# The second half of an output projection turned round: tokens on partitions, added and normalized piece by piece

## What is computed

```python
def rmsnorm(x, gain):
    y = x * lax.rsqrt(jnp.mean(x * x, axis=-1, keepdims=True) + RMS_EPS)
    return y * gain
...
mix = jnp.concatenate([y_rwkv, y_attn], axis=-1)   # 1024 x 2048
x = x + mix @ w_out[l]                             # w_out is 2048 x 2048
return rmsnorm(x, final_gain)
```

## Time and profile before

| | us |
|---|---|
| time, median of 3 runs | 1854.89 (1854.79 to 1863.19) |
| time of the profiled execution | 1853.96 |
| its span | 1852.0 |
| TensorE busy | 1821.9 (98%) |
| VectorE busy | 1242.8 (67%) |
| ScalarE busy | 815.3 (44%) |
| GpSimd busy | 476.8 (26%) |

### The profile page before, as it was taken

How to read it: one execution, slowest core, us unless ns; L and a number is a source line. 1 busy time by engine, 2 the same in 40 slices (tenths; PEclk the granted TensorE clock), 3 DMA queues, 4 the chain that set the end, 5 groups by cost and what they waited for, 6 DMA issues and landing times.

```text
span 1852.0 us, 37362 instructions
## 1 busy us (share of the span) xinstructions
PE 1821.9 (98%) x14560; PEld 1489.1 (80%) x14560; DVE 1242.8 (67%) x2239; ACT 815.3 (44%) x1690; POOL 476.8 (26%) x1096
## 2 busy tenths in 40 slices
PE   8999999999999999999999999999999999999996
PEld 5778888888888887888888888888888778888885
DVE  4676777777777678667777777787678753356433
ACT  6435444443535355444444535353544543242221
POOL 0005061423324150051423324050505060111110
PEclk9999999999999999999999999999999999999998
DMA  6533332333333335333433333333333543465433
GB/s 183 163 114 103 91 93 87 96 91 94 91 91 92 97 92 179 107 89 86 104 85 95 90 92 99 90 87 93 101 96 104 172 117 108 126 206 182 153 120 125
DMA packets 194960, 207.65 MB, mean 112 GB/s; under 512 B 98272, under 2 KB 101472, under 8 KB 194784
## 3 DMA queue, kind: packets, MB, share of 16 engines
q1 hardware_dynamic: 194784, 205.26, 38.9%
HBM read 183.18 MB, written 22.02 MB: 111 GB/s over the span
## 4 chain that ended last, share of the span: by engine, by line
PE 85%; POOL 4%; DVE 4%; DMA 3%; issue 2%; SPq 1%; ACT 1%; DVEq 0%; POOLq 0%; ACTq 0%
PE psum L1206 70%; PE psum L1191 3%; POOL sub_io L520 2%; POOL sub_t L518 2%; PE psum L1330 2%; PE psum L1270 1%; PE psum L1480 1%; PE psum L1298 1%; PE psum L1363 1%; PE psum L1444 1%; PE psum L1451 1%; DMA sub_l<-scratch_L 1%; PE psum L1215 1%; DMA w_raw<-in_w_in 1%; PE psum L1232 1%
## 5 line engine op out<-in xcount | busy, mean ns | idle before, releaser
L1206 PE MATMUL psum<-x_hi,w_hi 128*128 128x512 f32 x2144 | 870.7, 406 | 9.2 <-DVE x_lo L788 6.2
L1206 PE MATMUL psum<-x_hi,w_lo 128*128 128x512 f32 x2144 | 838.4, 391 | 0.0
L1206 PE MATMUL psum<-x_lo,w_hi 128*128 128x512 f32 x2144 | 838.0, 391 | 0.0
L779 DVE TENSOR_TENSOR w_lo<-w_raw,w_hi 128x512 fp32r<-128x512 f32 x536 | 372.5, 696 | 491.3 <-ACT w_hi L563 462.4
L563 ACT ACTIVATE w_hi<-w_raw 128x512 fp32r<-128x512 f32 x536 | 335.4, 629 | 740.2 <-PE psum L1206 631.8
L1206 PEld LDWEIGHTS psum<-x_hi,w_hi 128*128 128x128 f32 x2144 | 403.5, 188 | 108.5 <-issue 13.7
L1206 PEld LDWEIGHTS psum<-x_hi,w_lo 128*128 128x128 f32 x2144 | 403.0, 188 | 87.2
L1206 PEld LDWEIGHTS psum<-x_lo,w_hi 128*128 128x128 f32 x2144 | 404.0, 188 | 79.9 <-issue 4.4
L518 POOL TENSOR_TENSOR sub_t<-sub_l,sub_io 128x60 f32<-128x60 f32 (+24 forms) x496 | 192.8, 389 | 876.9 <-DMA sub_l<-scratch_L 839.3
L520 POOL TENSOR_TENSOR sub_io<-sub_io,sub_t 128x60 f32<-128x60 f32 (+24 forms) x496 | 199.1, 401 | 38.8
L540 POOL TENSOR_TENSOR v<-v,kb 128x512 f32<-128x512 f32 x29 | 38.2, 1316 | 265.1 <-ACT kb L723 264.7
(11 more groups left out here) (246 smaller groups left out, 1867.6 us busy)
## 6 DMA issues: line engine op xcount, KB each, us to landing
w_raw<-in_w_in SPq DMA_DIRECT2D x408, 256.0 KB, 2.7
w_raw<-in_w_out SPq DMA_DIRECT2D x128, 256.0 KB, 2.7
sub_l<-scratch_L SPq DMA_DIRECT2D x16, 512.0 KB, 4.6
stage<-in_x_t SPq DMA_DIRECT2D x20, 256.0 KB, 3.3
stage<-scratch_MIX SPq DMA_DIRECT2D x19, 256.0 KB, 3.9
late<-in_x_t SPq DMA_DIRECT2D x16, 256.0 KB, 3.2
scratch_MIX<-sa SPq DMA_DIRECT2D x16, 256.0 KB, 3.5
scratch_MIX<-ym SPq DMA_DIRECT2D x16, 256.0 KB, 3.2
```

The lines of the kernel that those rows point to most:

```text
L779: nc.vector.tensor_tensor(w_lo[gq % SPLIT][:], w_raw[gq % RAW][:], w_hi[gq % SPLIT][:].bitcast(F32), ALU.subtract).then_inc(w_ready, 1)
L1206: mm = nc.tensor.matmul(psum[:, s % 2], wt[gq % SPLIT][:, cols], xx[:, c], start=(c == 0 and wt is w_hi and xx is x_hi), stop=(c == KC - 1 ...
```

## The change

The second half of the output projection is turned round. Before, weights were the stationary operand and 512 tokens streamed; now a slice of 128 tokens of x is stationary and 512 output channels of the weights stream, so that tokens lie on partitions and the norm is a sum along the free dimension. A unit is now one slice of 128 of the depth (16 of them, `KC`) for one block of 512 output channels (`cb`, four of them), and for each token group (`tb`, four of them) three matmuls into a bank of its own; blocks take banks 4 to 7 and 0 to 3 in turn. A block of 128 tokens by 512 channels is a piece. The last block is made in two passes of two token groups each (`PASSES`), both of which load and split the block's weights again. There are thus 80 units behind `ROWS`, 48 of 12 matmuls and 32 of 6. In the last pass TensorE waits for all four last units and then does them for group 2 and afterwards for group 3 (`last_rows`).

A finished pass's pieces are added one by one, at every second unit of the next pass (`ADDED_AT`), each by VectorE, then squared with its row sum by ScalarE. GpSimd multiplies the pieces of blocks 0 to 2 by the gain; in block 3 the gain goes into the last scaling. Groups 0 and 1 are scaled at units 69 and 70, two pieces by ScalarE and two by VectorE, and stored from then on, one store per unit of SP's loop; groups 2 and 3 behind the last products.

```diff
-SEQS = OUT1 + KC
-QUARTERS = 4 * SEQS
+ROWS = 4 * OUT1
+CBS = D // HALF
+TBS = HALF // P
+PASSES = [(cb, range(TBS)) for cb in range(CBS - 1)] + [(CBS - 1, (0, 1)), (CBS - 1, (2, 3))]
+LAST_UNITS = 4
+QUARTERS = ROWS + KC * len(PASSES)
+PIECES = [(cb, tb) for cb, tbs in PASSES for tb in tbs]
+ADDED_AT = [ROWS + KC * (at + 1) + 1 + 2 * i for at, (_, tbs) in enumerate(PASSES[:-1]) for i in range(len(tbs))]
+FIRST_SCALED = ADDED_AT[-1] + 1
...
                 def load_w(gq):
...
+                    if gq < ROWS:
+                        s, part_ = quarter_at(gq)
+                        src = io["w_in"][s % H1, part_] if s < OUT0 else io["w_out"][s - OUT0, part_]
+                    else:
+                        at, c = divmod(gq - ROWS, KC)
+                        src = io["w_rows"][PASSES[at][0], c]
...
+                def residual_rows(n):
+                    cb, tb = PIECES[n]
+                    if n < 2:
+                        sp.wait_ge(tile_read, OUT0 + KC)
+                    else:
+                        sp.wait_ge(row_read, n - 1)
+                    sp.dma_start(x_in[n % 2], io["x_rows"][tb * P:(tb + 1) * P, cb * HALF:(cb + 1) * HALF]
+                                 ).then_inc(row_in_landed[n % 2], 16)
+                def store_rows(tb, cb):
+                    if cb < 2:
+                        sp.wait_ge(scaled_by_act, 2 * tb + cb + 1)
+                    else:
+                        sp.wait_ge(scaled_by_dve, 2 * tb + cb - 1)
+                    sp.dma_start(io["out_rows"][tb * P:(tb + 1) * P, cb * HALF:(cb + 1) * HALF], row_piece[tb][cb]
+                                 ).then_inc(out_stored, 16)
...
-                for t in range(KC):
-                    store(1, t)
+                    if gq == ROWS + 4:
+                        sp.wait_ge(x_ready, 4 * KC)
+                        sp.dma_start(gain_row, io["gain_row"]).then_inc(row_gain_landed, 16)
+                    if gq == ROWS + KC - 4:
+                        residual_rows(0)
+                        residual_rows(1)
+                    if gq - 1 in ADDED_AT:
+                        residual_rows(ADDED_AT.index(gq - 1) + 2)
...
+                    if gq >= QUARTERS - 2 * CBS:
+                        store_rows(*divmod(gq - (QUARTERS - 2 * CBS), CBS))
+                for tb, cb in ((2, 0), (2, 2), (2, 1), (2, 3), (3, 0), (3, 2), (3, 1), (3, 3)):
+                    store_rows(tb, cb)
                 sp.wait_ge(out_stored, 16 * 2 * KC)
...
+                def gain_rows(cb):
+                    pool.wait_ge(row_gain_landed, 16)
+                    for tb in range(TBS):
+                        pool.wait_ge(row_squared, TBS * cb + tb + 1)
+                        piece = row_piece[tb][cb]
+                        nc.gpsimd.tensor_tensor(piece, piece, gain_row[:, cb * HALF:(cb + 1) * HALF], ALU.mult
+                                                ).then_inc(row_gained, 1)
...
+                    for at in range(CBS - 1):
+                        if gq == ROWS + KC * (at + 1):
+                            gain_rows(at)
...
+                def square_rows(n):
+                    cb, tb = PIECES[n]
+                    act.wait_ge(row_read, n + 1)
+                    if n == 0:
+                        act.wait_ge(c_summed, KC)
+                    if n >= 2:
+                        act.wait_ge(row_squared, n - 1)
+                    nc.scalar.activation(c_sq[n % 2], row_piece[tb][cb], ACT.Square,
+                                         accum_out=row_sums[:, tb, cb:cb + 1]).then_inc(row_squared, 1)
+                def root_rows(tb):
+                    act.wait_ge(row_summed, tb + 1)
+                    nc.scalar.activation(row_inv[:, tb:tb + 1], row_inv[:, tb:tb + 1], ACT.Sqrt, bias=eps[:, 0:1],
+                                         scale=1.0 / D).then_inc(row_rooted, 1)
+                def scale_rows(tb):
+                    act.wait_ge(row_inverted, tb + 1)
+                    act.wait_ge(row_gained, TBS * (CBS - 1))
+                    for cb in range(2):
+                        copy(row_piece[tb][cb], row_piece[tb][cb], row_inv[:, tb:tb + 1]).then_inc(scaled_by_act, 1)
...
-                square(2 * KC - 1)
-                root(1)
+                    if gq in ADDED_AT:
+                        square_rows(ADDED_AT.index(gq))
+                    if gq == FIRST_SCALED:
+                        root_rows(0)
+                        root_rows(1)
+                    if gq - FIRST_SCALED in (1, 2):
+                        scale_rows(gq - FIRST_SCALED - 1)
+                for tb in (2, 3):
+                    square_rows(PIECES.index((CBS - 1, tb)))
+                    root_rows(tb)
+                    scale_rows(tb)
...
+                def add_rows(n):
+                    cb, tb = PIECES[n]
+                    if n == 0:
                         dve.wait_ge(mix_stored, 16 * INTERVALS)
-                    nc.vector.tensor_tensor(xn[h][t], psum[:, (OUT0 + u) % 2], x_in[u % 2], ALU.add
-                                            ).then_inc(tile_read, 1)
...
+                    dve.wait_ge(row_in_landed[n % 2], 16 * (n // 2 + 1))
+                    nc.vector.tensor_tensor(row_piece[tb][cb], psum[:, row_bank(cb, tb)], x_in[n % 2], ALU.add
+                                            ).then_inc(row_read, 1)
+                def sum_rows(tb):
+                    dve.wait_ge(row_squared, PIECES.index((CBS - 1, tb)) + 1)
+                    nc.vector.tensor_reduce(row_inv[:, tb:tb + 1], row_sums[:, tb], AX, ALU.add).then_inc(row_summed, 1)
+                def invert_rows(tb):
+                    dve.wait_ge(row_rooted, tb + 1)
+                    then(nc.vector.reciprocal(row_inv[:, tb:tb + 1], row_inv[:, tb:tb + 1]))
+                    dve.sem_inc(row_inverted, 1)
+                def scale_third(tb):
+                    dve.wait_ge(row_gained, TBS * (CBS - 1))
+                    nc.vector.tensor_scalar(row_piece[tb][2], row_piece[tb][2], row_inv[:, tb:tb + 1], None, ALU.mult
+                                            ).then_inc(scaled_by_dve, 1)
+                def scale_fourth(tb):
+                    nc.vector.scalar_tensor_tensor(row_piece[tb][3], row_piece[tb][3], row_inv[:, tb:tb + 1],
+                                                   gain_row[:, 3 * HALF:], ALU.mult, ALU.mult
+                                                   ).then_inc(scaled_by_dve, 1)
+                def scale_rows(tb):
+                    scale_third(tb)
+                    scale_fourth(tb)
...
-                add(2 * KC - 1)
-                invert(1)
-                dve.wait_ge(c_turned, 1)
-                for t in range(KC):
-                    scale(1, t)
...
+                    if gq in ADDED_AT:
+                        dve.wait_ge(w_used, ROWS + KC * ((gq - ROWS) // KC))
+                        add_rows(ADDED_AT.index(gq))
+                    if gq == FIRST_SCALED:
+                        sum_rows(0)
+                        sum_rows(1)
+                        invert_rows(0)
+                        invert_rows(1)
+                    if gq - FIRST_SCALED in (1, 2):
+                        scale_rows(gq - FIRST_SCALED - 1)
+                dve.wait_ge(row_full, 1)
+                add_rows(PIECES.index((CBS - 1, 2)))
+                sum_rows(2)
+                invert_rows(2)
+                scale_third(2)
+                dve.wait_ge(row_full, 2)
+                add_rows(PIECES.index((CBS - 1, 3)))
+                scale_fourth(2)
+                sum_rows(3)
+                invert_rows(3)
+                scale_rows(3)
...
+                def row_products(gq, tb, c, cb):
+                    bank = row_bank(cb, tb)
+                    tokens = slice(tb * P, (tb + 1) * P)
+                    hi, lo = w_hi[gq % SPLIT], w_lo[gq % SPLIT]
+                    nc.tensor.matmul(psum[:, bank], x_hi[:, c, tokens], hi[:], start=(c == 0), stop=False)
+                    nc.tensor.matmul(psum[:, bank], x_hi[:, c, tokens], lo[:], start=False, stop=False)
+                    return nc.tensor.matmul(psum[:, bank], x_lo[:, c, tokens], hi[:], start=False, stop=(c == KC - 1))
+                def rows(gq):
+                    at, c = divmod(gq - ROWS, KC)
+                    cb, tbs = PASSES[at]
...
+                    if at == 0:
+                        pe.wait_ge(x_ready, 3 * KC + c + 1)
+                    if at == 1 and c == 0:
+                        pe.wait_ge(tile_read, OUT0 + KC)
+                        pe.wait_ge(c_rooted, 1)
+                    if at in (2, 3) and c == 0:
+                        pe.wait_ge(row_read, TBS * (at - 1))
+                    pe.wait_ge(w_ready, gq + 1)
+                    for tb in tbs:
+                        mm = row_products(gq, tb, c, cb)
+                    mm.then_inc(w_used, 1)
+                def last_rows():
+                    cb, tbs = PASSES[-1]
+                    pe.wait_ge(w_ready, QUARTERS)
```

(73 more changed lines are left out.)

71 lines of the change are left out of this document (36 added, 35 removed).

## The result

Over 20 runs each the changed kernel took 1862.64 us at the median against 1858.0 before (three of these 20 are the ones shown ahead of the prediction, whose median was 1854.89). The ratio is 1.0025, with a 95% interval from 1.0015 to 1.0035. Forecast were 0.1% less and a range of 1845 to 1859. Against 0.5%, what the prediction called the least that can be told from no change, it is none; but the interval lies wholly above 1, so the small shift that there is goes upward, and not down as forecast.

What follows compares the result with a forecast made beforehand. The prediction took TensorE, busy for 98% of the span, to bound the kernel: 1852.0 - 0.8 (gap) - 10.7 (tail) + 9.3 (supply waiting) = 1849.8, plus 1.96 and 0.93 to the median, 1852.7 us; range 1845 to 1859.

Steps and rivals of the forecast that it cites:

- Matmuls and the start of the second half: Second half of the out-projection: TensorE's starting gap of 0.83 us goes; number and shapes of large matmuls stay, costing nothing.
- The tail: Behind TensorE's last product: falls from 18.4 to 7.7 us, 10.7 less, with bounds of 6.5 and 8.5.
- The weight supply: Loading and splitting weights in the 32 short units cannot make good lost time: 9.3 us of waiting added.
- the walk: Rule-by-rule timing of the 32 short units: TensorE waits at units 58 to 75 and 4.07 us before the last four.
- the two errors named above: For the last four units' wait, the walk had the last load issued at about 43.2 us and landing in 2.72.
- The rival of later landings: Short units: weight loads land later, from about 3.2 us on the kernel is slower than before; chance 0.11.
- the supply keep up: Rival for the short units: collisions and handovers are absorbed, the full 11.5 us show, 1843.4; chance 0.11.
- The clock: Rival: a bare 4 us wait ahead of the last 24 matmuls lowers the clock, up to 5.4 us more; chance 0.16.
- The base and the first 1660 us: The sum started from one span of 1852.0 and a median of 1854.89, with no difference ahead of the second half.

Runs made afterwards that it cites:

- a_warm: The changed kernel with 16 matmuls on data never used, issued where TensorE waits for the last four units; 1.0003 of the kernel before.
- a_each: The changed kernel with TensorE taking the last four units of group 2 one by one as they get ready; 0.9994 of the kernel before.
- b_shift: The kernel before with one unused buffer of 64 bytes per partition where the changed kernel has its row sums; 1.0013 of the kernel before.

## Why the prediction was wrong, step by step

The forecast was 1852.7 and the result 1862.6, 9.9 above. By the means, 3.1 of it are the base (1858.0 where the sum had 1854.89), 3.0 lie in the part behind the first half (0.8 more than before, where the sum had 2.2 less), and 3.8 in the changed kernel's first 1660 us.

- **Matmuls and the start of the second half**: right. No gap at the start, the pitch unchanged.
- **The tail**: 18.4 to 8.1, forecast 7.7. Right in kind; the last four stores were issued 3.2, 3.6, 4.1 and 4.6 us after the last matmul (1850.13), and landed in 2.4, 2.7, 3.0 and 3.1 us, so the last at 7.7 where the sum had 7.4; every store was put at 2.2.
- **The weight supply**: right in mechanism, place and size. 9.1 us of waiting against 9.3, at the units that the walk named, and six buffers left 2.5 of it where the same walk said 2.3. That the last wait came out so close is in part luck, by the two errors named above. The rival of later landings did not occur as such (2.7 at the median in the short units); only the last load, beside the early stores, took 3.5 us, and 4.1 and 4.2 in a_warm and a_each. Nor did the supply keep up.
- **The clock**: a step that failed, and the one that turned the sign in the part that the change touches. I had it as a rival at 0.16 and up to 5.4 us; with a bare wait of 4 us in my own walk and the fall in a gap shown by the earlier trace rows, it should have been a term of the sum. It cost 2.6 us. With it the forecast would have been 1852.4 for the span from this base, 0.4 above before; the measured part behind is 0.3 to 0.8 above.
- **The base and the first 1660 us**: the step that failed with the larger number. The sum starts from one trace of 1852.0 and a median of three runs, and it puts the difference between the kernels in the 1660 us ahead of the change at nothing, without a reason. That trace was a lucky one: with 7.1 us it has the least idle time of TensorE there among all 18, and its second half begins at 1657.7 where they run from 1656.9 to 1672.4. The median of 20 runs lay 3.1 higher, and the changed kernel carries some 4 us there that go with the place of its buffers. With the clock alone the forecast would have been 1855.3, still inside the range; base and first part took the result beyond its upper end.

## What to carry to other kernels

When a pass is cut into shorter units, compare the whole reload loop (split, handover, issue, landing, over the number of buffers) with the buffers' share of the new units: 4.13 against 4.08 us meant that every later delay stayed. A bare wait of TensorE of 4 us was paid twice, the second time in clock. Stagger the end by finishing whole units group by group, rather than by halving the units, and base the sum on more than one execution when the effect is a few tenths of a per cent.

## What the runs showed of the hardware that was not expected

The granted clock fell to 1.2 GHz in a wait of 4.1 us, and also where two waits of 1.3 us had three matmuls between them, and behind a single wait of 1.45 us in b_shift; in the changed kernel's trace it was back at 2.4 GHz at about 1847.3, with dense matmuls from 1842.1 on. Sixteen unused matmuls in the wait kept it at 1.00. Weight loads of 256 KB landed in 2.7 us at the median in the short units, at 180 GB/s from 1790 to 1835, but in 3.5 to 4.2 us when the early stores ran beside them (DMA share 1.05, 406 GB/s from 1839). And the same instructions, with their buffers 64 bytes further on, ran 4.1 us (give or take 1.7) longer in 1860.
